# First FFN of a two-block transformer kernel: half of the first weight panel ahead of x's second half, gate products first, modulation products half a step later

## The chip, the cores and the metric

The kernel runs on one NeuronCore of a Trainium2 chip. The metric is the device time of one execution in microseconds, taken as the median of several runs. TensorE, VectorE, ScalarE, GpSimd and the sync engine (SP) each run their own instruction list and meet only at semaphores; weights come from HBM through DMA queues that SP and GpSimd feed.

## The reference, cut to what matters

Two blocks over a sequence of 512 tokens with 1024 features. Only the first FFN and the modulation vector of the second block are touched:

```python
# block 1, first step; D_MODEL 1024, D_FF 2816
x = x + 0.5 * swiglu(rms_norm(x, ffn1_norm), ffn1_w_gate, ffn1_w_up, ffn1_w_down)
# swiglu(h): (silu(h @ w_gate) * (h @ w_up)) @ w_down
...
# block 2 scales and shifts by six 1024-wide parts of one vector
mod = silu(c) @ w_mod + b_mod          # w_mod: 1024 x 6144
```

The rest (gated MLP and differential attention, a second FFN, then the second block with a state-space part, windowed attention and a conv FFN) follows in one chain and is the same in both kernels.

## The kernel before

Features lie on partitions: x is 8 tiles (k = 0 to 7) of 128 features by 512 tokens. Every float32 operand of a product is split into a rounded part (`hi`) and the rest (`lo`), and each product is three TensorE products: hi by hi, hi by lo and lo by hi. Weights come in panels of 128 x 2048 (1 MB): SP loads one into one of two `w_raw` buffers, ScalarE casts it to `w_hi`, VectorE subtracts for `w_lo` (semaphore `w_split`), and only then may SP load the panel after next (`load`, L492: panel n waits for `w_split` of n - 1).

**Start.** SP issues x in four quarters of 256 features (L568), then gate panel 0 in two halves (L530, L531), then up panel 1 (L532), then many small parameter loads, panel 2, the small spread loads of `load_spread` (L510), and panel 3. TensorE transposes x tile by tile into PSUM banks 2 to 5 (L2521); VectorE copies each tile to `x` (L1663); ScalarE makes `h_hi` = x times the norm's gain (L828), VectorE `h_lo` (L1376). The norm's root is applied later, to the products. Between the transposes and the products TensorE multiplies ones (`idle_products`, L2507). ScalarE casts the first half of panel 0 behind six of the eight `h_hi` tiles (L920), and the second half behind the seventh (L923).

**First FFN.** It has 11 steps of two panels (gate, then up), each panel 48 products of 512 columns: 8 k, 2 output tiles, 3 terms. `first_gate` (L2353) runs panel 0 by terms: 16 hi by hi, 16 hi by lo, 16 lo by hi; then `first_sums` (L2525) transposes parameter rows, multiplies the position table and sums the squares of x for the root. Later panels go through `by_k` (L2336). VectorE's step (L1567 to L1594) is: scale two gate tiles by the root, split the next gate panel, multiply silu by two up tiles, split the next up panel, make two `hid_lo` tiles.

**Modulation.** Beside the first FFN, the first 8 of 12 groups of mod (512 columns each) are made. GpSimd loads eight tiles of w_mod per group into four buffers (`group`, L623): a buffer is loaded again once VectorE has used it (`mod_step`). VectorE multiplies and adds (`modulation`, L1539) at the head of each step: for step 0 four products ahead of the root and four behind the split of panel 2, for the others all eight. At the end of the step TensorE adds up the partitions with 4 small products (8 records, L2394), for which it waits until all eight are done. GpSimd starts group 0's last four loads only behind `cleared` (L647), which waits for the position table's copy on VectorE (L1674, behind `first_sums`) and clears a tile; the table copies of `tables` (L655) follow in the same queue.

`PHASES` cuts the steps into loops: 0; 1 to 6; 7; 8 to 10. The same `swiglu`, `gate_up` and `modulation` serve the second FFN, with a column of conditions on its name.

Of the kernel before, what the change touches and what calls it, by code (L numbers as in the profile page):

```python
# [33 lines left out]
P = 128  # L34
T = 512
TB = T // P
# [41 lines left out]
PHASES = {"ffn1": ((0, 1, True, None), (1, BESIDE_STEPS - 1, True, None), (BESIDE_STEPS - 1, BESIDE_STEPS, True, None), (BESIDE_STEPS, GU_STEPS, False, None)),  # L78
# [57 lines left out]
def build(nc, inp, rel_onehot, out):  # L136
# [13 lines left out]
    with ExitStack() as ctx:  # L150
# [135 lines left out]
        SW_BEFORE = [sum(len(k) for k in SW_BLOCKS[:u]) for u in range(len(SW_UNITS) + 1)]  # L286

# [203 lines left out]
        def _(sp):  # L491
# [32 lines left out]
            def load_ffn(name, gate, up, gate_col, up_col, down):  # L524
# [3 lines left out]
                if base == 0:  # L528
                    first_panel = panel(w_raw, 0, KD, PC)
                    sp.dma_start(first_panel[:, 0:KD // 2], gate_v[:, 0:KD // 2, 0:PC]).then_inc(S("w0_tables_landed"), 16)  # L530
                    sp.dma_start(first_panel[:, KD // 2:], gate_v[:, KD // 2:, 0:PC]).then_inc(S("w_landed0"), 16)  # L531
# [35 lines left out]
            for q in range(D // PC):  # L567
                sp.dma_start(x_in[:, :, q * PC:(q + 1) * PC], x_v[:, :, q * PC:(q + 1) * PC]).then_inc(S(f"x_landed{q}"), 16)  # L568
# [194 lines left out]
        def _(act):  # L763
# [153 lines left out]
            first_hi = lambda ks: scaled_hi("n1", "start", lambda k: gain1[:, k:k + 1], ks)  # L917
# [424 lines left out]
        def _(dve):  # L1342
# [210 lines left out]
            def swiglu(name):  # L1553
                base = BASE[name]
                setup = (s5_matrices, s5_first_angles, s5_second_angles, s5_powers)
                for start, stop, mods, extra in PHASES[name]:
                    if start == BESIDE_STEPS:
# [9 lines left out]
                    with dve.Fori(start, stop) as i:  # L1567
                        if start == 0:
                            modulation(i + MOD_AT[name], i, range(MOD_SLOTS))
                            refined_root({"ffn1": "n1", "ffn2": "n2"}[name])  # L1570
                        elif mods:
                            modulation(i + MOD_AT[name], i, range(KD if name == "ffn1" else MOD_SLOTS))
# [9 lines left out]
                        if start == 0 and name == "ffn1":  # L1582
                            modulation(i + MOD_AT[name], i, range(MOD_SLOTS, KD))
# [77 lines left out]
            for k in range(KD):  # L1661
                dve.wait_ge(S("x_t"), k + 2)
                dve.tensor_copy(x[:, k, :], B[2 + k % 4][:]).then_inc(S("x_turned"), 1)  # L1663
                if k == 3:
                    scaled_lo("n1", lambda k: gain1[:, k:k + 1], (0, ))
            scaled_lo("n1", lambda k: gain1[:, k:k + 1], range(1, KD))
            split(0)
            split(1)
            dve.wait_ge(S("rows_t"), 3)
# [569 lines left out]
        def _(pe):  # L2239
# [113 lines left out]
            def first_gate(n, banks, h_name, between):  # L2353

                wh, wl = panel(w_hi, n, KD, PC), panel(w_lo, n, KD, PC)
                if h_name == "n1":
                    pe.wait_ge(S("w0_begun"), 1)
                else:
                    pe.wait_ge(S("w_hi_done"), n + 1)
                for wait, h in ((ready_hi, h_hi), (ready, h_lo)):  # L2360
                    for k in range(KD):
                        wait(h_name)(k)
                        if h_name == "n1" and h is h_hi and k == KD // 2:
                            pe.wait_ge(S("w_hi_done"), n + 1)
                        for t, bank in enumerate(banks):
                            pe.matmul(bank[:], wh[:, k, t * P:(t + 1) * P], h[:, k, :], start=k == 0 and h is h_hi, stop=False)  # L2366
                if h_name != "n1":
                    between()
# [6 lines left out]
                if h_name == "n1":  # L2375
                    between()

            def gate_up(name, h_name, free, sums=None):

                base = BASE[name]  # L2380
                for start, stop, mods, extra in PHASES.get(name, ((1, GU_STEPS, False, None),)):
                    with pe.Fori(start, stop) as i:
# [752 lines left out]
```

## Time and profile before

| | us |
|---|---|
| median of 3 runs (lowest, highest) | 1749.19 (1748.01, 1749.32) |
| profiled execution, its own time | 1748.42 |
| its span, first to last record | 1746.8 |
| TensorE busy | 1736.5 (99%) |
| VectorE, ScalarE, GpSimd busy | 1057.1, 736.4, 199.4 |
| first weight product starts | 13.97 |
| step 1 of the first FFN starts | 39.43 |

Times in the rows are microseconds from the start of the span; PE is TensorE (PEld its weight loads), DVE is VectorE, ACT is ScalarE, POOL is GpSimd, and SPq is SP's sequencer, where DMA issues stand. A float32 transpose or product of 128 columns is recorded as two instructions or as one according to its kind, so counts of the trace and of the code can differ by a factor of two. A matmul's recorded duration includes its way through the array, so 16 in a row take less than 16 durations.

### The profile page before, as it was taken

The page shows a single profiled execution, that of the slowest core. Times are in us where ns is not written, and L with a number is a line of the kernel's source. Part 1 is how long each engine was busy: PE and PEld are TensorE (multiplying, and loading weights), DVE is VectorE, ACT ScalarE, POOL GpSimd, SP SyncE. Part 2 cuts the span into 40 slices and gives each one's busy share as a digit, 9 for nine tenths or more (in the row PEclk, how much of TensorE's full clock was granted, in tenths as well). Part 3 has the DMA queues.
Part 4 walks back from the last instruction along what each step waited for, and adds up shares of the span by engine and source line. Part 5 has one row for each costly group of instructions (what it writes and reads, how often), then busy time and mean ns, then how long its engine had stood idle before and what let it go on. Part 6 is the DMA issues. An engine that isn't in the chain of part 4 may idle for free.

```text
span 1746.8 us, 23624 instructions
## 1 busy us (share of the span) xinstructions
PE 1736.5 (99%) x8907; PEld 1425.0 (82%) x8907; DVE 1057.1 (61%) x1623; ACT 736.4 (42%) x1045; POOL 199.4 (11%) x249
## 2 busy tenths in 40 slices
PE   9999999999999999999999999999999999999999
PEld 7888888888888777788888888888987888888887
DVE  6666536655564667655788854346587665555423
ACT  5322223333444887623333322224576455555321
POOL 2222001140000000004510120130003300000000
PEclk9999999999999999999999999999999999999999
DMA  7877422343223211223754562325131222222331
GB/s 246 251 227 226 139 75 82 102 150 103 97 65 104 66 56 49 73 97 97 235 181 135 161 175 66 103 96 193 49 147 49 97 97 96 96 96 84 102 116 67
DMA packets 169701, 207.18 MB, mean 119 GB/s; under 512 B 18516, under 2 KB 144850, under 8 KB 169106
## 3 DMA queue, kind: packets, MB, share of 16 engines
q1 hardware_dynamic: 142882, 161.97, 28.6%
q0 software_dynamic: 12752, 38.81, 7.1%
q10 hardware_dynamic: 13984, 5.27, 1.4%
q8 instruction: 55, 0.90, 0.2%
q14 instruction: 28, 0.23, 0.0%
HBM read 190.56 MB, written 17.56 MB: 119 GB/s over the span
## 4 chain that ended last, share of the span: by engine, by line
PE 94%; DVE 3%; DMA 2%; ACT 1%; issue 0%; POOL 0%; SPq 0%; ACTq 0%; DVEq 0%
PE bank L2348 41%; PE bank L2275 35%; PE bank L2666 5%; PE bank L2690 1%; PE bank L2787 1%; DMA w_raw<-in_w_in 1%; PE bank L2243 1%; PE bank L2366 1%; PE bank L2700 1%; PE bank L2560 1%; PE bank L3048 1%; PE bank L2840 0%; PE bank L3060 0%; PE bank L2909 0%; PE bank L2372 0%; PE bank L2854 0%
## 5 line engine op out<-in xcount | busy, mean ns | idle before, releaser
L778 ACT CAST w_hi<-w_raw 128x2048 fp32r<-128x2048 f32 x154 | 294.1, 1910 | 722.4 <-PE bank L2348 355.5
L1356 DVE TENSOR_TENSOR w_lo<-w_raw,w_hi 128x2048 fp32r<-128x2048 f32 x156 | 364.7, 2338 | 348.0 <-ACT w_hi L778 347.3
L2348 PE MATMUL bank<-h_hi,w_hi 128*128 128x512 f32 x1024 | 400.7, 391 | 0.5 <-DVE h_lo L1397 0.2
L2348 PE MATMUL bank<-h_hi,w_lo 128*128 128x512 f32 x1024 | 398.6, 389 | 0.0
L2348 PE MATMUL bank<-h_lo,w_hi 128*128 128x512 f32 x1024 | 315.4, 389 | 0.0
L2348 PEld LDWEIGHTS bank<-h_hi,w_hi 128*128 128x128 f32 x1024 | 192.2, 188 | 44.6 <-issue 3.3
L2348 PEld LDWEIGHTS bank<-h_lo,w_hi 128*128 128x128 f32 x1024 | 192.2, 188 | 40.2
L2348 PEld LDWEIGHTS bank<-h_hi,w_lo 128*128 128x128 f32 x1024 | 192.2, 188 | 39.2
L2275 PE MATMUL bank<-hid_hi,w_hi 128*128 128x512 f32 (+1 forms) x450 | 173.3, 385 | 0.0
L2275 PE MATMUL bank<-hid_lo,w_hi 128*128 128x512 f32 (+1 forms) x450 | 172.9, 384 | 0.0
L2275 PE MATMUL bank<-hid_hi,w_lo 128*128 128x512 f32 (+1 forms) x450 | 172.9, 384 | 0.0
L670 POOL TENSOR_TENSOR tmp<-x 128x512 f32<-128x512 f32 x28 | 43.3, 1548 | 623.6 <-DVE x L1978 312.2
L2275 PEld LDWEIGHTS bank<-hid_hi,w_hi 128*128 128x128 f32 x450 | 84.5, 188 | 17.0
L2275 PEld LDWEIGHTS bank<-hid_hi,w_lo 128*128 128x128 f32 x450 | 84.5, 188 | 16.9
L2275 PEld LDWEIGHTS bank<-hid_lo,w_hi 128*128 128x128 f32 x450 | 84.5, 188 | 16.6
L2275 PE MATMUL bank<-w_hi,h_hi 128*128 128x512 f32 (+1 forms) x240 | 91.2, 380 | 0.3 <-DVE w_lo L1356 0.3
L2275 PE MATMUL bank<-w_hi,h_lo 128*128 128x512 f32 (+1 forms) x240 | 90.1, 375 | 0.0
L2275 PE MATMUL bank<-w_lo,h_hi 128*128 128x512 f32 (+1 forms) x240 | 90.0, 375 | 0.0
L1550 DVE SCALAR_TENSOR_TENSOR mod_acc<-mod_raw,small,mod_acc 128x512 f32<-128x512 f32 x84 | 63.1, 751 | 27.3 <-DMA mod_raw<-in_w_mod 22.6
L627 POOL DMA_DIRECT2D mod_raw<-in_w_mod x96 | 52.0, 543 | 171.2 <-DVE mod_acc L1547 123.2
L1592 DVE TENSOR_TENSOR tmp<-tmp,bank 128x512 f32<-128x512 f32 x44 | 28.2, 683 | 70.7 <-PE bank L2348 70.7
L2203 DVE SCALAR_TENSOR_TENSOR tmp<-bank,vec,tmp 128x511 f32<-128x511 f32 x88 | 63.8, 745 | 6.4 <-DVE tmp L2203 1.7
(506 smaller groups left out, 2690.9 us busy)
## 6 DMA issues: line engine op xcount, KB each, us to landing
w_raw<-in_w_in SPq DMA_DIRECT2D x29, 1024.0 KB, 5.1
mod_raw<-in_w_mod POOLq DMA_DIRECT2D x96, 256.0 KB, 4.8
w_raw<-in_ffn_w_up SPq DMA_DIRECT2D x22, 1024.0 KB, 5.6
w_raw<-in_w_up SPq DMA_DIRECT2D x22, 1024.0 KB, 5.1
w_raw<-in_ffn_w_gate SPq DMA_DIRECT2D x21, 1024.0 KB, 6.7
w_raw<-in_ffn_w_down SPq DMA_DIRECT2D x16, 768.0 KB, 4.3
w_raw<-in_ffn_w_down SPq DMA_DIRECT2D x16, 640.0 KB, 3.9
w_raw<-in_w_out SPq DMA_DIRECT2D x8, 1024.0 KB, 4.9
```

The lines of the kernel that those rows point to most:

```text
L627: pool.dma_start(mod_raw[:, k % MOD_SLOTS, :], wm[:, k, bass.ds(i * T + first * T, T)])\
L670: done(pool.tensor_tensor(tmp[:, min(k, 1), :], x[:, k, :], x[:, k, :], ALU.mult))
L778: act.copy(w_hi[i % 2][:], w_raw[i % 2][:]).then_inc(S("w_hi_done"), 1)
L1356: dve.tensor_tensor(w_lo[s][:], w_raw[s][:], w_hi[s][:].bitcast(F32), ALU.subtract).then_inc(S("w_split"), 1)
L1550: ins = dve.scalar_tensor_tensor(mod_acc[:], mod_raw[:, k % MOD_SLOTS, :], small[:, k:k + 1], mod_acc[:], ALU.mult, ALU.add)
L1592: dve.tensor_tensor(tmp[:, 2 + t, :], tmp[:, t, :], B[2 + t][:], ALU.mult).then_inc(S("hid"), 1)
L2203: dve.scalar_tensor_tensor(y[:, back:], up[:, :T - back], col_at(f"conv_w_2:{2 - back}", i * 2, KF * half + t), y[:, back:], ALU.mult, ALU ...
L2243: mm = pe.matmul(out_ap, stationary, moving, start=first and i == 0, stop=last and i == len(terms) - 1)
L2275: mm = pe.matmul(out_ap, stationary, moving, start=first and i == 0, stop=last and i == total - 1)
L2348: mm = pe.matmul(bank[:], w[:, k, at], h[:, k, :], start=k == first and part == 0 and i == 0, stop=k == last and part == 1)
L2366: pe.matmul(bank[:], wh[:, k, t * P:(t + 1) * P], h[:, k, :], start=k == 0 and h is h_hi, stop=False)
L2666: mm = pe.matmul(beside_bank(name, t)[:], stationary, moving, start=j == 0, stop=j == 3 * k - 1)
```

## The change

SP: x comes as quarters (0, 1), then x's second half in one load; the first half of panel 0 is issued ahead of x's second half, the second half of the panel behind it. The four transposed tiles of x's second half get banks 4 to 7. ScalarE makes `h_hi` straight from the transposed tile's bank; VectorE copies the tile to `x` after it. The panel's first half is cast after four tiles instead of six, and its `lo` half gets a subtraction of its own. TensorE transposes four tiles, runs the first half's hi by hi products, transposes the other four, and runs the rest of panel 0; the six idle products behind the transposes go (the eight at the very start stay). Panel 1's hi by hi products come ahead of `first_sums`.

Modulation in the first FFN: group 0's first four products stay ahead of step 0, but behind `split(1)`, and the other four come at the end of step 0. Groups 1 to 7 come behind the gate panel's split of their step instead of at its head. TensorE's small products of group g move from the end of step g to the middle of step g + 1, behind its gate panel.

```diff
-PHASES = {"ffn1": ((0, 1, True, None), (1, BESIDE_STEPS - 1, True, None), (BESIDE_STEPS - 1, BESIDE_STEPS, True, None), (BESIDE_STEPS, GU_STEPS, False, None)),
+PHASES = {"ffn1": ((0, 1, True, None), (1, 2, True, None), (2, BESIDE_STEPS, True, None),
+                   (BESIDE_STEPS, BESIDE_STEPS + 1, False, None), (BESIDE_STEPS + 1, GU_STEPS, False, None)),
...
+        X_QUARTERS = ((0, 2), (2, 4), (4, KD))
+        def x_bank(k):
+            return B[k if k >= 4 else 2 + k]
...
+                    load_x(0)
+                    load_x(1)
+                    sp.dma_start(gate_panel[:, early], gate_v[:, early, 0:PC]).then_inc(S("w0_tables_landed"), 16)
+                    load_x(2)
+                    sp.dma_start(gate_panel[:, late], gate_v[:, late, 0:PC]).then_inc(S("w_landed0"), 16)
...
+                for k in ks:
+                    act.wait_ge(S("x_t"), k + 2)
+                    act.activation(h_hi[:, k, :], x_bank(k)[:], ACT.Identity, scale=gain1[:, k:k + 1]).then_inc(S("norm_hi"), 1)
...
-            first_hi(range(6))
+            first_hi(range(4))
             act.wait_ge(S("w0_tables_landed"), 16)
-            act.copy(w_hi[0][:, 0:PANEL // 2], w_raw[0][:, 0:PANEL // 2]).then_inc(S("w0_begun"), 1)
-            first_hi((6, ))
+            act.copy(w_hi[0][:, early], w_raw[0][:, early]).then_inc(S("w0_begun"), 1)
+            first_hi(range(4, KD))
             act.wait_ge(S("w_landed0"), 16)
-            act.copy(w_hi[0][:, PANEL // 2:], w_raw[0][:, PANEL // 2:]).then_inc(S("w_hi_done"), 1)
-            first_hi((7, ))
+            act.copy(w_hi[0][:, late], w_raw[0][:, late]).then_inc(S("w_hi_done"), 1)
...
                         if start == 0:
-                            modulation(i + MOD_AT[name], i, range(MOD_SLOTS))
+                            if name == "ffn2":
+                                modulation(i + MOD_AT[name], i, range(MOD_SLOTS))
...
                         split(i * 2 + (base + 2), base)
-                        if start == 0 and name == "ffn1":
-                            modulation(i + MOD_AT[name], i, range(MOD_SLOTS, KD))
+                        if mods and start and name == "ffn1":
+                            modulation(i + MOD_AT[name], i)
...
                         split(i * 2 + (base + 3), base + 1)
                         for t in range(2):
                             hid_lo_of(name, i, t, 2 + t)
+                        if start == 0 and name == "ffn1":
+                            modulation(i + MOD_AT[name], i, range(MOD_SLOTS, KD))
...
+            first_x(range(4))
+            first_lo(range(4))
+            dve.wait_ge(S("w0_begun"), 1)
+            low_part(slice(0, PANEL // 2), "w_lo_begun")
+            first_x(range(4, KD))
+            first_lo(range(4, KD))
+            dve.wait_ge(S("w_hi_done"), 1)
+            low_part(slice(PANEL // 2, PANEL), "w_split")
             split(1)
+            modulation(0, 0, range(MOD_SLOTS))
...
+            def first_ffn_step():
+                early, late = range(KD // 2), range(KD // 2, KD)
+                turned_x(early)
+                pe.wait_ge(S("w0_begun"), 1)
+                first_products(0, early, w_hi, h_hi, ready_hi)
+                turned_x(late)
+                first_products(0, early, w_hi, h_lo, ready)
+                pe.wait_ge(S("w_lo_begun"), 1)
+                first_products(0, early, w_lo, h_hi, ready_hi)
+                pe.wait_ge(S("w_hi_done"), 1)
+                first_products(0, late, w_hi, h_hi, ready_hi)
+                first_products(0, late, w_hi, h_lo, ready)
+                pe.wait_ge(S("w_split"), 1)
+                first_products(0, late, w_lo, h_hi, ready_hi)
+                pe.wait_ge(S("w_hi_done"), 2)
+                pe.wait_ge(S("x_turned"), 3)
+                first_products(1, range(KD), w_hi, h_hi, ready_hi)
+                first_sums()
+                first_products(1, range(KD), w_hi, h_lo, ready)
+                pe.wait_ge(S("w_split"), 2)
+                first_products(1, range(KD), w_lo, h_hi, ready_hi)
...
+                def modulation_rows(step, behind, first, last):
+                    pe.wait_ge(S("mod_step"), step * MOD_STEPS + ((MOD_AT[name] + behind + 1) * MOD_STEPS + MOD_SLOTS))
...
+                    if name == "ffn1" and start == 0:
+                        first_ffn_step()
+                        continue
...
+                            if name == "ffn1" and half == 0 and start <= BESIDE_STEPS:
+                                modulation_rows(i, -1, start == 1, start == BESIDE_STEPS)
...
-            idle_products(6, ones[:], 7)
```

`first_products(half, ks, w, h, wait)` issues for each k of ks one product for each of the half's two banks, each 512 columns wide, waiting for `h`'s tile k; `turned_x(ks)` transposes the tiles ks and for k = 4 and 5 waits until VectorE has copied tile k - 2.

## Rows read from the trace of the kernel before

**Rows 1.** The granted clock of TensorE in 40 slices of the span, in tenths of full speed.
```profile
PEclk9999999999999999999999999999999999999999
```

**Rows 2.** TensorE's longest wait after the start: who for whom, total, times, longest.
```profile
PE bank L2366 <- ACT w_hi L920: 0.9, 1, 0.9
```

**Rows 3.** Chain of waits, first 320 us: start, length, what.
```profile
13.97 7.55 PE bank L2366 x32
...
25.16 0.27 PE bank L2531 x3
...
38.04 0.76 DVE mod_acc L1550
38.84 0.43 PE bank L2394 x8
...
61.83 21.99 PE bank L2348 x96
```

**Rows 4.** Timeline of TensorE: first product of panel 1, step 1's gate and up panel.
```profile
27.01 0.47 PE L2348 MATMUL bank<-h_hi,w_hi 128*128 128x512 f32 x1
...
39.43 0.49 PE L2348 MATMUL bank<-h_hi,w_hi 128*128 128x512 f32 x1 [0.16 <-issue]
...
50.43 0.39 PE L2348 MATMUL bank<-h_hi,w_hi 128*128 128x512 f32 x1
```

**Rows 5.** TensorE's transposes grouped, 5.9 to 9.3 us, then 9.8 to 11.5 us.
```profile
L2521 PE MATMUL bank<-ident,x_in 128*128 128x128 f32 x16 | 3.7, 424 | 0.0
...
L2521 PE MATMUL bank<-ident,x_in 128*128 128x128 f32 x16 | 2.3, 306 | 0.0
```

**Rows 6.** Timeline of ScalarE and VectorE, 5.9 to 27 us.
```profile
9.67 0.69 DVE L1663 COPY x<-bank 128x512 f32<-128x512 f32 x1 [0.16 <-PE bank L2521]
...
12.89 1.03 ACT L920 CAST w_hi<-w_raw 128x1024 fp32r<-128x1024 f32 x1
```

**Rows 7.** VectorE and ScalarE grouped, 7 to 26 us: busy, mean ns, idle before.
```profile
L1376 DVE SCALAR_TENSOR_TENSOR h_lo<-x,gain,h_hi 128x512 fp32r<-128x512 f32 x8 | 5.5, 743 | 0.0
...
L828 ACT ACTIVATE h_hi<-x,gain 128x512 fp32r<-128x512 f32 x8 | 5.7, 720 | 2.1 <-DVE x L1663 1.7
```

**Rows 8.** One load each, issue to landing: x's third quarter with its second; panel's first half.
```profile
L568 SPq DMA_DIRECT2D x_in<-in_x x2: 494/497/500, 1.5 to 2.1; - x2
...
DMA to landing us min/median/max: 4.5/5.5/6.6
...
L530 SPq DMA_DIRECT2D w_raw<-in_ffn_w_gate x1: 593/593/593, 3.2 to 3.2; - x1
...
DMA to landing us min/median/max: 8.5/8.5/8.5
```

**Rows 9.** Timeline of SP: loads of panels 2 and 3.
```profile
20.27 0.40 SPq L500 DMA_DIRECT2D w_raw<-in_ffn_w_gate  x1
...
28.81 2.71 SPq L500 DMA_DIRECT2D w_raw<-in_ffn_w_up  x1
```

**Rows 10.** Panel 3, then panel 2: their loads' time from issue to landing.
```profile
DMA to landing us min/median/max: 13.6/13.6/13.6
...
DMA to landing us min/median/max: 8.2/8.2/8.2
```

**Rows 11.** Timeline of VectorE behind panel 3, and of four modulation products later.
```profile
44.34 2.29 DVE L1356 TENSOR_TENSOR w_lo<-w_raw,w_hi 128x2048 fp32r<-128x2048 f32 x1 [4.36 <-ACT w_hi L778]
46.55 1.28 DVE L1426 TENSOR_TENSOR hid_lo<-tmp,hid_hi 128x512 fp32r<-128x512 f32 x2
...
71.98 3.12 DVE L1550 SCALAR_TENSOR_TENSOR mod_acc<-mod_raw,small,mod_acc 128x512 f32<-128x512 f32 x4 [2.18 <-DMA mod_raw<-in_w_mod]
```

**Rows 12.** Timeline of GpSimd: group 0's last four loads.
```profile
28.55 2.14 POOL L627 DMA_DIRECT2D mod_raw<-in_w_mod  x4 [0.30 <-POOL zero L650]
```

**Rows 13.** DMA queues, 35 to 39 us: q0 is GpSimd's, q1 SP's; packets, MB, share.
```profile
q0 software_dynamic: 356, 1.08, 72.3%
q1 hardware_dynamic: 434, 0.44, 31.7%
```

More of the change, by code:

```diff
@@ L1660, in _, with first_x, first_lo, low_part @@
             dve.tensor_copy(gain1[:], B[6][:, 0:2 * KD]).then_inc(S("x_turned"), 1)
[L1661 to L1667, printed above, removed]
+            def first_x(ks):
+                for k in ks:
+                    dve.wait_ge(S("norm_hi"), k + 1)
+                    dve.tensor_copy(x[:, k, :], x_bank(k)[:]).then_inc(S("x_turned"), 1)
+            def first_lo(ks):
+                for k in ks:
+                    dve.wait_ge(S("x_turned"), k + 2)
+                    scaled_lo("n1", lambda k: gain1[:, k:k + 1], (k, ))
+            def low_part(at, signal):
+                dve.tensor_tensor(w_lo[0][:, at], w_raw[0][:, at], w_hi[0][:, at].bitcast(F32), ALU.subtract).then_inc(S(signal), 1)
+            first_x(range(4))
[6 more added lines that the diff above has]
+            low_part(slice(PANEL // 2, PANEL), "w_split")
             split(1)
+            modulation(0, 0, range(MOD_SLOTS))
             dve.wait_ge(S("rows_t"), 3)
@@ L2362, in first_gate @@
                         wait(h_name)(k)
-                        if h_name == "n1" and h is h_hi and k == KD // 2:
-                            pe.wait_ge(S("w_hi_done"), n + 1)
                         for t, bank in enumerate(banks):
                             pe.matmul(bank[:], wh[:, k, t * P:(t + 1) * P], h[:, k, :], start=k == 0 and h is h_hi, stop=False)
-                if h_name != "n1":
-                    between()
+                between()
                 pe.wait_ge(S("w_split"), n + 1)
@@ L2374, in first_gate, with turned_x @@
                             mm.then_inc(S("pe_done"), 2)
-                if h_name == "n1":
-                    between()
+            def turned_x(ks):
+                for k in ks:
+                    pe.wait_ge(S(f"x_landed{min(k // 2, 2)}"), 16)
+                    if k in (4, 5):
+                        pe.wait_ge(S("x_turned"), k)
+                    for b in range(TB):
+                        mm = pe.transpose(x_bank(k)[:, b * P:(b + 1) * P], x_in[:, b, k * P:(k + 1) * P], ident[:])
+                    mm.then_inc(S("x_t"), 1)
@@ new lines, in first_products @@
+            def first_products(half, ks, w, h, wait):
+                weights = panel(w, half, KD, PC)
+                for k in ks:
+                    wait("n1")(k)
+                    for t in range(2):
+                        mm = pe.matmul(B[2 * half + t][:], weights[:, k, t * P:(t + 1) * P], h[:, k, :], start=k == 0 and w is w_hi and h is h_hi,
+                                       stop=k == KD - 1 and w is w_lo)
+                        if k == KD - 1 and w is w_lo:
+                            mm.then_inc(S("pe_done"), 2)
@@ L2378, in gate_up @@
             def gate_up(name, h_name, free, sums=None):
                 base = BASE[name]
+                def modulation_rows(step, behind, first, last):
+                    pe.wait_ge(S("mod_step"), step * MOD_STEPS + ((MOD_AT[name] + behind + 1) * MOD_STEPS + MOD_SLOTS))
+                    for j in range(4):
+                        mm = pe.matmul(B[6][32 * j:32 * j + 32, 0:P], row_of[:], mod_acc[:, j * P:(j + 1) * P], start=first, stop=last)
+                    mm.then_inc(S("mod_acc_free"), 1)
@@ L2542, in swiglu_free @@
                 return free
-            gate_up("ffn1", "n1", swiglu_free("ffn1"), first_sums)
+            gate_up("ffn1", "n1", swiglu_free("ffn1"))
             down("ffn1")
```

37 lines of the change are left out of this document (12 added, 25 removed).

## The prediction

> **What bounds the kernel now.** Look first at the waits of TensorE and at the granted clock: TensorE is busy for 99% of the span (the table above) at full clock [rows 1], and after its start nothing stops it for more than 0.9 us at a time [rows 2]. So a change of order can only win what TensorE waits for, and the chain of waits of the first 60 us says where that is. Before 13.97 us it goes through x's copies and casts. From there to 38 us it is weight products, with `first_sums` in between. Then come four modulation products on VectorE, 0.76 us each, and the eight small products that waited for them [rows 3]. Step 1 starts at 39.43 and its up panel at 50.43 [rows 4], and from then on each step is 96 products in 21.99 us and 0.36 us of small products without a gap [rows 3]. The whole argument is therefore one number: by how much does step 1's up panel start earlier or later than 50.43? What is late there is late at the end.
>
> **The earlier start.** The first product waits for the cast of half a panel, 12.89 to 13.92 [rows 6], behind six `h_hi` tiles. Now four go ahead of it, and ScalarE reads the bank itself. The fourth tile is in its bank at 9.67, where VectorE's copy starts today [rows 6]; plus 0.72 for `h_hi` [rows 7] and 1.03 for the cast: 11.4, first product 11.5. The half panel must be there by 10.4. It takes the slot of x's third quarter, which landed 6.6 us after 2.1, so at 8.7; with today's 8.5 us from issue [rows 8] it would be 10.6. Both bounds cost at most 0.2. Gain 2.5 us.
>
> What is paid for it: the 16 transposes of x's second half now stand between products. In the first 3.4 us of transposes sixteen take 3.7 us, later sixteen take 2.3, tail of 0.3 included [rows 5]: I take 2.0. The 96 products of step 0 go at the pace of the 48 from 13.97 to 25.16 [rows 3], 0.227 each after the first's latency, 21.9 in all. `first_sums` takes 25.16 to 27.01 [rows 3, 4], 1.9. So the up panel ends at 11.5 + 2.0 + 21.9 + 1.9 = 37.3, against 38.0 now. The small products no longer stand there, nor does the wait for them: step 1 starts at 37.4 instead of 39.43, a gain of 2.0. Inside it everything is covered: the second half's `h_hi` (16.9), its cast (18.0) and panel 1's (19.9) are made before TensorE wants them (19.2, 19.2 and 24.5).
>
> Behind `first_sums` (end 30.0) come the root, its refinement, two scaled gates and the split of panel 2, about 6.7 us together as today from 27.3 to 35.4 less the modulation products that stood in between. That is 36.7, just ahead of 37.4. If this cover goes, the time lost is hidden by the next paragraph's wait.
>
> **The new wait.** Step 1's gate panel takes 11.0 us [rows 4], so TensorE is through it at 48.4. There it now waits for all eight products of group 0, and VectorE makes the last four of them only behind step 0's split of panel 3 and two `hid_lo` tiles. Today they are made at 35.5 to 38.8, ahead of that split. So a load whose split had 3.8 us of slack (done at 46.6 [rows 11], wanted at 50.43) comes onto the path with the products behind it: panel 3. Behind the waiting products in TensorE's queue stands the whole up panel; behind that split in VectorE's queue stand step 1's gates too.
>
> When does panel 3 land? Its load is the last of a row of issues on SP: panel 2 goes out at 20.27, the moment panel 0's `w_split` comes, and panel 3 8.54 us later, with the small spread loads between [rows 9]. VectorE's new order up to that `w_split`: the copies of tiles 0 to 3 wait for `h_hi` and end at 9.67 + 0.72 + 0.69 = 11.1; then VectorE is never idle: four `h_lo` at 0.68 (5.5 / 8) [rows 7], half a split 1.15, four copies 2.8, four `h_lo` 2.7, half a split 1.15: 21.6. Panel 2 goes out 1.3 us later than now and panel 3 at 30.1. It took 13.6 us to land [rows 10], so 43.7.
>
> From landing to TensorE: cast 1.94 (42.4 to 44.34), split until `hid_lo` at 46.55, so 2.2, two `hid_lo` 1.2, four products 3.1 [rows 11] with 0.1 ahead, and 0.6 from the last product to the first weight product behind the small ones, as now (38.80 to 39.43) [rows 3, 4]. That is 9.1. The up panel of step 1 starts at 43.7 + 9.1 = 52.8 instead of 50.43: a loss of 2.4 us. TensorE stands still from 48.4 to 52.2, nearly 4 us, where it stood 0.7 before.
>
> Bounds of the load's 13.6. Below: panel 2's took 8.2 [rows 10]; panel 3 then lands at 38.3 and nothing waits. Above: in 35 to 39 us GpSimd's queue carried 1.08 MB and SP's 0.44 [rows 13], so panel 3 gets a quarter or less of the engines while group 0's last loads and the table copies run. GpSimd's four loads started at 28.55, ahead of panel 3 [rows 12]. They wait for the table's copy behind `first_sums`, now 3 us later, so up to 2 us more of them meets the panel, at three quarters of the engines: 1 to 1.5 us more. On the other side, group 1's loads, which took part of the engines before 42.4, now wait for VectorE. I take 13.6, the same load's own row, since both shifts are small and opposed.
>
> **The rest of the modulation move.** Steps 1 to 7 keep all their instructions. VectorE's eight products come behind a split of 2.3 instead of ahead of two gates; with their wait for loads they took 8 us and end within a microsecond of the up panel's end, and what needs them, the small products, has another 11 us. The scaled gates come earlier. I cost this at nothing; the cover is half a step, and each microsecond beyond it would count seven times. The small products are as many as before (8 groups, 0.36 us each in the chain). GpSimd's group and table queue moves with VectorE, half a step later, and its last copies have over a step until ScalarE waits for them. The cut of the loops costs nothing: the chain shows no gap at the cuts of today.
>
> **Sum.** Step 1's up panel +2.4, the rest 0. The profiled execution took 1748.42, so 1750.8 by it; the median of the runs shown is 0.8 above that execution, which would make 1751.6. I predict 1751.2.
>
> **Rivals.**
>
> A. *Not slower: panel 3 lands early.* The new wait is nothing if the panel has landed by 48.4 + 0.4 - 9.1 = 39.7, and costs less than the gain if by 41.3, which is 11.2 us from issue. For it: GpSimd's loads start later and group 1's do not come, so the panel could have the engines to itself at first. Against: it is itself queued behind the spread loads, which now run 1.3 us later, and 13.6 included more than 3 us before its data moved at all. Then the up panel starts at 48.8, a gain of 1.6: 1747.2 with half the offset to the median.
>
> B. *The clock is low at the start.* The six idle products and the copies' pace kept TensorE at work to 13 us. Now it stands still from 9.9 to 11.5. The transposes ran at half pace at first (0.23 each) and at full pace from about 9.6 [rows 5], so at the 1.2 GHz level and then at 2.4. If the rise comes later in the new order, the first eight products take 1.8 us more and the late transposes 1.6 more; copies, `w_split` and panel 3 move by some 2 us: +4.5, 1753.3. For it: the rise came only at the very end of the stretch of work that is now all there is before the pause. Against: that stretch itself is unchanged.
>
> C. *The clock falls in the new wait.* No row here has TensorE idle for 4 us, and no row has the clock fall [rows 1, 2]. If it falls, some products of the up panel take twice 0.227; 8 to 16 of them are 1.8 to 3.6 us: +5, 1753.8.
> The Trainium skill ("TensorE: Matmul & The Clock Gate", "Part 1: The HAM clock gate") says that the array's clock is let up by sustained work and goes back to 1.2 GHz in idleness. It speaks for B and C; that rows 5 show the rise agrees with it, and no row here shows the fall.
>
> D. *The panel is later still*, by GpSimd's loads meeting it or by the half panel of the start landing late: +4, 1752.8.
>
> **Chances.** Forecast 0.50; A 0.20; B 0.12; C 0.08; D 0.10. What a measurement of this kernel can tell from no change is 0.2%, 3.5 us: under 1745.7 or over 1752.7. No case reaches the first, and a misjudged gain gets 0.03. Over the second lie most of B and C, half of D and a little of the forecast's spread: 0.22. The rest, 0.75, is within. The range takes in A and half of B to D: 1746.8 to 1753.9; the forecast's own is 1750 to 1752.5.
>
> **What would show it.** In the profile after: the first product at 11.5 (later with the half panel's landing as releaser: the load order did not help; transposes and products at twice their spacing: B). Step 1's gate panel at 37.4. Panel 3's issue at 30.1 and its cast at 43.7. A wait of 3 to 4 us of TensorE's small products for the modulation product on VectorE, once, and none in steps 2 to 8. If that wait is missing I am wrong in the sign; if it recurs in each step, in the size.

## The result, and the profile after

The changed kernel takes 1755.38 us (median of 6 executions, 1750.80 to 1758.88); the kernel before, run beside it on the same chip, 1747.87. The ratio is 1.0043, with a 95% interval of 1.0034 to 1.0053: slower by 7.5 us, where 1751.2 was predicted and, with a chance of 0.75, a difference of less than 0.2%. All times below are medians of such executions; kernels that were run together share the runs of the kernel before.

The six executions differ in one more thing: their mean granted clock is 0.996 to 0.999, and the longest are those with the lowest clock. The kernel before keeps 1.000 nearly always. The execution that was profiled is the fastest, 1750.80 with a span of 1749.3; a second profile of the same kernel took 1754.18. Both are shown, as their difference is part of the answer.

TensorE's waits in the first profile (who for whom, total, times, longest), against 0.9 after the start in [rows 2]:

```profile
PE bank L2917 <- issue: 3.1, 1, 3.1
PE bank L2428 <- ACT w_hi L942: 1.9, 1, 1.9
PE bank L2593 <- POOL ones L630: 1.3, 1, 1.3
PE bank L2464 <- DVE mod_acc L1571: 1.1, 1, 1.1
```

The last row is the wait that was predicted. The first was in no step of mine: 3.1 us in which nothing that the profile shows was waited for. TensorE's timeline (start, length, what, idle before and releaser):

```profile
5.28 3.04 PE L2419 MATMUL bank<-ident,x_in 128*128 128x128 f32 x16
10.18 3.15 PE L2428 MATMUL bank<-h_hi,w_hi 128*128 128x512 f32 x8 [1.85 <-ACT w_hi L942]
13.12 2.52 PE L2419 MATMUL bank<-ident,x_in 128*128 128x128 f32 x16
...
37.58 0.39 PE L2391 MATMUL bank<-h_hi,w_hi 128*128 128x512 f32 x1
49.71 0.43 PE L2464 MATMUL bank<-mod_acc,row_of 128*32 128x128 f32 x8 [1.08 <-DVE mod_acc L1571]
1282.38 3.91 PE L2917 MATMUL bank<-uc,wb 64*64 64x64 f32 x127
1289.37 0.27 PE L2917 MATMUL bank<-uc,wb 64*64 64x64 f32 x1 [3.08 <-issue]
```

These rows answer to [rows 4, 5]. The first product starts at 10.18 instead of 13.97, step 1 at 37.58 instead of 39.43. The last two rows are over a millisecond later, in a part that the change does not touch: 128 small products (L2917) run without a gap in the kernel before, and here the last of them stands alone behind the 3.1 us. The same place in the kernel before (L2840), where the last of the 128 is sent between the first two of the next group:

```profile
1282.90 4.12 PE L2840 MATMUL bank<-uc,wb 64*64 64x64 f32 x127
1286.81 0.27 PE L2898 MATMUL bank<-tz,uc 64*64 64x128 f32 x1
1286.86 0.22 PE L2840 MATMUL bank<-uc,wb 64*64 64x64 f32 x1
```

The chain of waits for the place that the prediction turns on (start, length, what; it answers to [rows 3, 10, 11]):

```profile
29.11 11.84 DMA w_raw<-in_ffn_w_up
...
40.97 1.92 ACT w_hi L793
...
42.92 1.07 DVE w_lo L1377
...
45.12 1.28 DVE hid_lo L1447 x2
...
48.90 0.76 DVE mod_acc L1571
...
49.71 0.43 PE bank L2464 x8
50.13 21.98 PE bank L2391 x96
```

The path is the predicted one, link by link. Here the panel came after 11.84 us and the up panel starts at 50.13, 0.3 before the old 50.43. The chain passes `PE bank L2402`, the end of the first FFN, at 261.43 in the kernel before and at 261.19 (L2488) in this execution: up to there nothing is lost. All of its 2.5 us come from the wait at 1286. In the kernel's second profile the same chain reads:

```profile
28.07 14.01 DMA w_raw<-in_ffn_w_up
...
50.83 0.65 PE bank L2464 x8
51.48 23.88 PE bank L2391 x96
75.72 21.99 PE bank L2391 x96
```

and its windows (stretch in us, its length, TensorE's busy time and instructions, granted clock, mean busy share of the DMA engines, GB/s):

```profile
42.00:46.40 4.40, 4.34 (x20) 1.00 0.33 108
46.40:50.80 4.40, 0.00 (x0) 0.76 0.75 236
50.80:54.80 4.00, 3.97 (x16) 0.50 0.75 266
54.80:58.80 4.00, 4.00 (x17) 0.91 0.84 259
```

Here the panel needs 14.01 us and TensorE stands still for 4.49 us. From 48.7, still inside this wait, the granted clock is 0.50, the 1.2 GHz level, for 6.8 us: the 96 products take 23.88 us instead of the 21.99 of [rows 3]. This execution passes the end of the first FFN at 264.43, 3.0 late, and loses another 2.8 at 1289 to 1293. So there are two losses of about 3 us, of which I had priced the first at 2.4 and the second at nothing.

### The profile page after: what moved, and what is told of

Same layout as the page of the kernel before. It is cut to its first block, busy times and chain, and to the rows that moved or that the text cites. A ratio compares the mean times of both kernels' runs of the same rounds, so it can differ in the third digit from the quotient of the medians.

```text
span 1749.3 us, 23597 instructions
## 1 busy us (share of the span) xinstructions
PE 1735.7 (99%) x8895; PEld 1424.1 (81%) x8895; DVE 1057.7 (60%) x1624; ACT 735.9 (42%) x1045; POOL 199.2 (11%) x249
## 4 chain that ended last, share of the span: by engine, by line
PE 94%; DVE 3%; ACT 1%; DMA 1%; issue 1%; SPq 0%; POOL 0%; DVEq 0%; POOLq 0%
PE bank L2391 40%; PE bank L2318 35%; PE bank L2743 5%; PE bank L2767 1%; PE bank L2864 1%; PE bank L2286 1%; PE bank L2777 1%; DMA w_raw<-in_ffn_w_up 1%; PE bank L2637 1%; PE bank L3125 1%; PE bank L2832 0%; PE bank L2917 0%; PE bank L3137 0%; PE bank L2986 0%; PE bank L2931 0%
## 5 line engine op out<-in xcount | busy, mean ns | idle before, releaser
L2391 PE MATMUL bank<-h_hi,w_hi 128*128 128x512 f32 x1008 | 394.3, 391 | 0.4 <-DVE h_lo L1418 0.4
L2391 PE MATMUL bank<-h_hi,w_lo 128*128 128x512 f32 x1008 | 392.4, 389 | 0.0
L2391 PE MATMUL bank<-h_lo,w_hi 128*128 128x512 f32 x1008 | 310.4, 389 | 0.0
L2391 PEld LDWEIGHTS bank<-h_lo,w_hi 128*128 128x128 f32 x1008 | 189.2, 188 | 39.5
L1600 DVE TENSOR_TENSOR tmp<-bank,rstd 128x512 f32<-128x512 f32 x44 | 28.3, 686 | 55.9 <-PE bank L2391 48.0
```

Of the source, the lines that this page charges most:

```text
L1600: dve.tensor_tensor(tmp[:, t, :], B[t][:], rstd[:], ALU.mult).then_inc(S("gate_scaled"), 1)
L2391: mm = pe.matmul(bank[:], w[:, k, at], h[:, k, :], start=k == first and part == 0 and i == 0, stop=k == last and part == 1)
```

## The experiments

**Is it repeatable?** The changed kernel once more, beside the third set.

> The changed kernel itself once more, for a second profile and more times. Clock theory: wherever its mean clock is 0.996 to 0.998, the profile shows the clock at half behind the wait of the small products (about 50 us), behind the issue wait at the state-space inputs (about 1288 us), or both, for some 7 us each; none elsewhere but in the pause of the start. Median 1754 to 1757, 6 to 10 us above before. Rival (the slow executions are slow somewhere else): a wait or a low clock in another place.

Measured: 1754.82, ratio 1.0048 [1.0034, 1.0061], clocks 0.996 to 0.998. Its profile is the second one above, and shows both losses in one execution.

**Is it the pause at the start?** Two runs: the changed kernel with eight idle products between the first four tiles and the first weight product (e1, "filled"); and the reverse, the old kernel without its six (e2).

```diff
# e1_filled, against the changed kernel
                 turned_x(early)
+                idle_products(8, ones[:], 7)
                 pe.wait_ge(S("w0_begun"), 1)
# e2_before_no_idle, against the kernel before
-            idle_products(6, ones[:], 7)
```

> The changed kernel with one line more: eight idle products of ones (16 records) behind the transposes of x's first half, where TensorE stood still from 8.3 to 10.2 us. Clock theory (the pause lets TensorE's granted clock fall to half while the first products run; executions with a mean clock of 0.996 to 0.998 had it low for longer): mean clock 0.999 to 1.000 in every execution, the spread of 8 us gone, time 4 to 7 us below the changed kernel's 1755.4, so within 3 us of before. Wait theory (the small products' wait for panel 3 is what is long in the slow executions): the time stays at 1753 to 1757 with the same spread. Layout theory (an issue wait of 3.1 us at the state-space inputs, L2917 of the changed kernel, because its instructions lie elsewhere): that wait stays, as the code is only a few instructions longer, and keeps the time 3 us above before.

> The kernel before without its six idle products between the transposes and the first product: the only thing done is that TensorE pauses from 11.6 to 14.0 us. Clock theory: clock under 1.000 in most executions, time 2 to 7 us above before, with a wide spread. Wait and layout theories: nothing else moves, so the same as before, within 0.5 us.

Measured: filled, 1757.18, 1.0053 [1.0039, 1.0066], clocks still 0.996 to 0.998; the old kernel without its six, 1747.76, 1.0000 [0.9991, 1.0009]. The pause is not the cause of the loss. The clock is full through the start of the filled kernel's profile, and its low clock shows in and behind the two other waits:

```profile
PE bank L2465 <- DVE mod_acc L1571: 4.2, 1, 4.2
PE bank L2918 <- issue: 3.5, 1, 3.5
```

For 6.8 us from 49.5 and for 6.8 us from 1291.9 it is granted half. That it is no faster than the changed kernel although its start is better was the first sign that the place of the code counts.

**Which half of the change?** The new start with the old modulation, and the old start with the new modulation (both with the phases that go with the modulation).

```diff
# e3_start_only, against the changed kernel: groups at the head of their step again
-                            if name == "ffn2":
-                                modulation(i + MOD_AT[name], i, range(MOD_SLOTS))
+                            modulation(i + MOD_AT[name], i, range(MOD_SLOTS))
...
                         first_ffn_step()
+                        modulation_rows(0, 0, True, False)
# e4_mod_only, against the kernel before: small products behind the next gate panel
+                            if name == "ffn1" and half == 0 and 1 <= start <= BESIDE_STEPS:
+                                modulation_rows(i, -1, start == 1, start == BESIDE_STEPS)
```

> The changed start (load order, transposes in two halves, panel 0 by halves, panel 1's first products ahead of the sums, no idle products) with the modulation as before: four products ahead of the root, four behind the split of panel 2, small products at the end of their own step. Clock theory: 1753 to 1757 with the wide spread and clocks of 0.996 to 0.999, as the pause is there. Wait theory: there is no wait for panel 3 any more, so about before's time, 0 to 1 us less.

> The start of before with the changed modulation: group 0's last four products behind the split of panel 3, the others behind the gate panel's split, small products in the middle of the next step. Clock theory: clock 1.000 and a narrow spread; only the wait for panel 3 counts: step 1 starts 1.4 us earlier, its up panel at 51 to 52, so 0 to +2 us against before. Wait theory: +4 to +8 us, as in the changed kernel, with its spread.

Measured: start only, 1752.19, 1.0025 [1.0016, 1.0035]; modulation only, 1753.92, 1.0036 [1.0024, 1.0048]. Either half alone loses, and for different reasons. The time of start only lies between what the two theories expected, so neither was right about it. It waits 4.2 us for group 0 ahead of step 1, gets half the clock for 3.4 us from 39.5, and has no wait for issue:

```profile
PE bank L2459 <- DVE mod_acc L1570: 4.2, 1, 4.2
```

So the start gives nothing while step 1 stands behind group 0's small products: the modulation has to move for it. Modulation only waits 0.8 us for group 0 and is 1.3 us ahead of the kernel before at the end of the first FFN (260.17 against 261.43). Its loss is at the other end:

```profile
1281.96 3.56 PE L2850 MATMUL bank<-uc,wb 64*64 64x64 f32 x115
...
1288.91 1.00 PE L2850 MATMUL bank<-uc,wb 64*64 64x64 f32 x13 [3.38 <-issue]
```

The gap now stands behind 115 products, not 127. What these kernels differ in at this place is only how many instructions TensorE's list has ahead of it: against the kernel before, modulation only has 198 more, the changed kernel 173 more, the filled one 205 more. The gap stands behind 115, 127 and 111 records: one record earlier for two instructions more. In the traces TensorE's instructions are fetched in packets of 16384 bytes, so a block's border should lie at a fixed count of the list, and whatever cuts a loop once more moves it. The next two runs test this.

**Is it the place of the code alone?** The kernel before with nothing changed but one more cut of TensorE's loop list (198 instructions more ahead of that place); and the changed kernel with three more cuts (782 more than the kernel before).

```diff
+CUTS = {"ffn1": (10,), "ffn2": ()}                 # e5_before_shifted
+CUTS = {"ffn1": (7, 10), "ffn2": (10,)}            # e6_after_shifted
...
-                for start, stop, mods, extra in PHASES.get(name, ((1, GU_STEPS, False, None),)):
+                for start, stop, mods, extra in PE_PHASES.get(name, ((1, GU_STEPS, False, None),)):
```

`PE_PHASES` is `PHASES` with each range cut at these steps. TensorE executes the same products in the same order.

> The kernel before with TensorE's list alone made longer: the loop over steps 8 to 10 of the first FFN is cut in two (8, 9 and 10), so one more unrolled step stands in the list, and everything behind it lies 198 instructions later (the changed kernel's lies 173 later). The same instructions run in the same order. Layout theory (the issue wait at the state-space inputs comes from where the list's blocks end, and the clock falls behind it): TensorE waits 3.0 to 3.5 us for issue at L2840 inside the second run of 128 small products, about 13 before its end as in e4_mod_only, the granted clock falls behind it in part of the executions, and the time is +3 to +7 us. Wait theory (only the modulation's waits count): no change, within 0.5 us.

> The changed kernel with three more cuts of TensorE's loops (the first FFN's steps 2 to 7 cut before 7, its last two steps and the second FFN's last three cut once each), so that the second block's code lies 782 later than in before, 14 more than three blocks of 256. The same instructions in the same order as in the changed kernel. Layout theory: no issue wait at the state-space inputs, time 3 to 6 us below the changed kernel's 1755.4, so 1749 to 1752; what is left is the wait for panel 3 and the clock behind it. Wait theory: 1755.

Measured: the kernel before, shifted, 1752.32, 1.0026 [1.0016, 1.0036]; 5.0 us for a loop cut. The changed kernel, shifted, 1751.42, 1.0016 [1.0007, 1.0025], 3.4 to 4.0 us under the changed kernel's two medians. (By the ratios, which take in two low executions of the eleven, 1747.87 and 1746.63, it is 4.7 or more.) In the shifted old kernel TensorE's timeline and windows (columns as above) show the gap and what follows it:

```profile
1282.16 3.59 PE L2845 MATMUL bank<-uc,wb 64*64 64x64 f32 x115
...
1289.07 1.01 PE L2845 MATMUL bank<-uc,wb 64*64 64x64 f32 x13 [3.32 <-issue]
```

```profile
1281.00:1285.00 4.00, 4.00 (x106) 1.00 1.02 341
1285.00:1289.00 4.00, 0.75 (x25) 0.91 0.65 208
1289.00:1293.00 4.00, 3.93 (x54) 0.50 0.02 4
1293.00:1297.00 4.00, 4.00 (x45) 0.74 0.00 0
```

TensorE stands still for 3.3 us, and for 6.8 us from 1288.3, shortly before it goes on, the clock is half. In the changed kernel, shifted, no wait for issue is left, but the wait for group 0 is 3.9 us and the clock is half for 6.8 us from 49.0.

**Why does the fetch take so long?** When TensorE comes to that place, the DMA engines are full (1.02 above). SP has queued 2 MB of `ca_out` and 2 MB for `w_out` behind 2 MB of `tz`. The run is the shifted old kernel again, with the `ca_out` load, and with it the `w_out` loads behind it, held back until that block of products is through:

```diff
+            sp.wait_ge(S("bu"), 2)
             sp.dma_start(ca_out[:], ca_dram[:]).then_inc(S("ca_landed"), 16)
```

> e5_before_shifted (before with a list 198 instructions longer) with one wait more on SP: the 2 MB load of ca_out, and the two 1 MB weight panels queued behind it, start only when TensorE is through the second run of 128 small products. Data theory (the list's next block of 256 instructions comes by DMA and is late because 6 MB of loads are in its way): the issue wait of 3.3 us at L2845 is gone, under 0.5 us; in its place the products that need ca_out wait some us for it, so the time is no better than e5's. Rival (the block is late by the list's form alone, whatever the data): the wait of 3.3 us stays where it is.

Measured: the gap is 0.31 us, at the same record.

```profile
1283.58 3.56 PE L2846 MATMUL bank<-uc,wb 64*64 64x64 f32 x115
...
1287.46 0.62 PE L2846 MATMUL bank<-uc,wb 64*64 64x64 f32 x13 [0.31 <-issue]
...
1295.99 5.38 PE L2915 MATMUL bank<-ca_out,tmp 64*64 64x128 f32 x64 [3.34 <-DMA ca_out<-chunk_outputs]
```

The fetches themselves are in the traces. TensorE's instruction packet of 16384 bytes stands in the queue q8: first the shifted old kernel, 1286 to 1287 us, then this run, 1285 to 1286 us.

```profile
q8 instruction: 1, 0.02, 7.0%
...
q8 instruction: 1, 0.02, 5.8%
```

In the first TensorE stops at 1285.75; the packet starts only at 1286.65, 0.9 us later, and lands at 1287.77, and the products go on at 1289.07. In the second the packet starts at 1285.09, 2.1 us ahead of the stop. Counted from the start of the 128 products, the packet moves 3.0 us later with the loads in the queues (4.5 against 1.5 us), which is the difference of the two gaps (3.32 less 0.31). In all seven profiles with a gap 1.3 to 1.5 us pass between the packet's landing and the next product. Why the transfer starts late, whether the fetch is asked for late or stands in line behind the loads, no record shows.

The time did not fall (1753.53, 1.0035 [1.0022, 1.0049]), as the last row says: the load held back is now waited for itself, 3.3 us, again with half the clock behind it. So the cause of the gap is shown, but holding the load back is no remedy. The Trainium skill ("Runtime: NRT & Kernel Launch", "Instruction fetch mechanics") says that the sequencer refills its buffer in 16 KiB blocks by a DMA queue of its own, at a cost that is mostly hidden. The traces agree with the block and with the queue; with idle DMA engines 0.31 us is nearly hidden, with full ones the 3.1 to 3.5 us are not.

**Is the rest group 0 behind panel 3?** The changed kernel with the last four products of group 0 ahead of panel 3's split.

```diff
+                        if start == 0 and name == "ffn1":
+                            modulation(i + MOD_AT[name], i, range(MOD_SLOTS, KD))
                         split(i * 2 + (base + 3), base + 1)
                         for t in range(2):
                             hid_lo_of(name, i, t, 2 + t)
-                        if start == 0 and name == "ffn1":
-                            modulation(i + MOD_AT[name], i, range(MOD_SLOTS, KD))
```

> The changed kernel with group 0's last four modulation products on VectorE ahead of the split of panel 3 instead of behind it and the two hid_lo tiles (VectorE is idle from 38.8 to 42.9 us there). Its code is as long as the changed kernel's. Wait theory: TensorE's small products wait for nothing, step 1's up panel starts at 48.7 instead of 50.1 to 53, and the clock no longer falls there: 2 to 4 us below the changed kernel. Layout theory: the issue wait of 3.1 us stays at the state-space inputs, with the clock's fall behind it in part of the executions, so not under 1749.

Measured: 1750.27, 1.0013 [1.0004, 1.0022]: 4.6 to 5.1 us less than the changed kernel, with the wait for issue (3.4) still in. In its profile no wait for group 0 is left, and the up panel starts at 49.04. Group 0 behind the split costs the changed kernel 4.6 to 5.1 us, more than the 2 to 4 that were expected.

**How much of it is the clock?** The changed kernel as in e6, with TensorE kept at work on idle products while it waits for group 0, and with one more cut, so that the list (1034 more) again has no border there.

```diff
+CUTS = {"ffn1": (7, 10), "ffn2": (9, 10)}
...
+                            if name == "ffn1" and half == 0 and start == 1:
+                                idle_products(14, ones[:])
                             if name == "ffn1" and half == 0 and start <= BESIDE_STEPS:
                                 modulation_rows(i, -1, start == 1, start == BESIDE_STEPS)
```

> e6_after_shifted (1751.4; no issue wait at the state-space inputs) with fourteen idle products ahead of the small products that wait for group 0 in step 1, so TensorE multiplies ones for 3.4 us of its wait of 3.9. The code of the second block lies 10 instructions later than in before modulo 256. If half of what this wait costs is the clock that falls behind it (6.8 us at half, 3.4 us lost): 1748 to 1749, mean clock 0.999 to 1.000. If the wait alone costs: the same as e6_after_shifted, or a little more.

Measured: 1749.28, 1.0010 [1.0001, 1.0019], against 1751.42 for e6: 2.1 us less. TensorE is not earlier for it: the idle products fill 3.1 us in the profile and the up panel starts at 51.81 against 51.09 in e6, but the products behind run at full pace. The same stretch, without the idle products (e6) and with them (e11):

```profile
46.00:50.00 4.00, 0.53 (x3) 0.88 0.72 217
50.00:54.00 4.00, 3.56 (x15) 0.50 0.89 306
```

```profile
46.00:50.00 4.00, 4.00 (x28) 1.00 0.47 131
50.00:54.00 4.00, 4.00 (x32) 1.00 1.04 364
```

In the chains the 96 products behind the wait take 24.28 us in e6 and 22.01 in e11, whose step 1 begins no earlier. So about 2 us of what group 0's wait costs are the clock's, and the rest is the wait itself.

**All together.** Eight idle products, the four modulation products early, and TensorE's list cut so that no border falls there (1028 instructions more); and the same without the idle products (996 more).

```diff
+CUTS = {"ffn1": (6, 7, 10), "ffn2": (10,)}
...
+                idle_products(8, ones[:], 7)               # e8_all only
...
                         # and group 0's last four ahead of split(panel 3), as in e7
```

> The changed kernel with the three put together: eight idle products in the pause of the start, group 0's last four products ahead of the split of panel 3, and TensorE's loops cut so that the second block's code lies 4 instructions later than in before, modulo 256. If the issue wait with its clock, the wait for panel 3 with its clock, and the pause of the start are the whole of it: mean clock 1.000 in every execution, no wait of TensorE over 1 us, step 1's up panel at 48 to 48.7 instead of 50.43, and 1.5 to 2.5 us below before. If something else of the change costs time: above before still.

> e8_all without its eight idle products, so TensorE pauses for 1.9 us in the start again. Clock theory: the clock falls to half from about 11 us on in part or all of the executions, mean clock 0.999 in these; the first products take twice as long and the whole is 0.5 to 2 us above e8_all's 1745.5. Rival (the idle products are worth nothing, as e2_before_no_idle found of the six in before): the same as e8_all within 0.3 us.

Measured: 1745.52 (1744.88 to 1746.33, 11 executions), 0.9985 [0.9976, 0.9994], clock 1.000 in all of them; without the idle products 1746.63, 0.9994 [0.9985, 1.0003], clock 0.999 in 5 of 11. The first is faster than both kernels, if by less than the 0.2% that count here. Its start:

```profile
7.70 1.95 PE L2599 MATMUL bank<-ones 128*128 128x128 f32 x16
10.01 2.12 PE L2433 MATMUL bank<-h_hi,w_hi 128*128 128x512 f32 x8 [0.35 <-ACT w_hi L947]
```

and its chain:

```profile
35.96 10.88 PE bank L2396 x48
46.84 0.36 PE bank L2470 x8
47.20 12.92 PE bank L2396 x56
```

The up panel starts at 47.20 against 50.43 in [rows 4]: the 3.2 us that the start really gains. The end of the first FFN is 3.2 us earlier too (258.26 against 261.43), the span is 2.6 shorter. The median is only 1.8 under that of the kernel before, as the profiled execution of the latter (1748.42) was 1.1 above the median of the runs beside e8, and that of e8 only 0.3 above its own.

| kernel | us | ratio [95%] | wait for group 0 | wait for issue |
|---|---|---|---|---|
| changed | 1755.38, 1754.82 | 1.0043 [1.0034, 1.0053], 1.0048 [1.0034, 1.0061] | 1.1, 4.5 | 3.1, 3.1 |
| e6, list shifted | 1751.42 | 1.0016 [1.0007, 1.0025] | 3.9 | none |
| e7, four early | 1750.27 | 1.0013 [1.0004, 1.0022] | none | 3.4 |
| e10, both | 1746.63 | 0.9994 [0.9985, 1.0003] | none | none |
| e8, both and filled | 1745.52 | 0.9985 [0.9976, 0.9994] | none | none |

e6 and e7 each take one loss away, e10 both. The two effects add, as far as the medians tell: 3.6 (e7 less e10) and 4.8 (e6 less e10) make 8.4, and from e10 to the changed kernel it is 8.2 to 8.8.

## Why the prediction was wrong

It said 1751.2 and the kernel takes 1755.38. **The step that failed** is the sentence "The cut of the loops costs nothing: the chain shows no gap at the cuts of today". I looked for the cost of a cut at the cut. It lies 1.25 ms later: the new phases and the new start lengthen TensorE's list by 173 instructions, the border of a 16384-byte block comes to lie in a dense run of small products while 6 MB of loads fill the DMA engines, and TensorE stands for 3.1 us. In neither profile of the changed kernel does the clock fall there, but in e1, e4 and e5 it does; a mean clock of 0.996 in some of the changed kernel's executions, as in the profile of e1 that has both falls, suggests that it does in these too. Price: 5.0 us where it is alone (e5 against the kernel before), 3.4 to 4.0 within the change (e6 against the changed kernel's medians). That is the larger part of the miss. The miss is also larger than 1755.38 less 1751.2: I had taken 1748.8 for the kernel before, and its runs here give 1747.87, so +2.4 was forecast and +7.5 measured. That the changed kernel without the shift stands at 1751.42, next to the 1751.2 predicted, is in part luck: it is 4.1 over its own before. The profile before held no number for the shift, but it has instruction packets among its DMA queues, and any change of the list's length moves every border: the upper bound should not have been zero.

**A term was mis-sized**: the new wait. Its mechanism was right in each link: from the panel's landing to the up panel I worked out 9.1 us, and they are 9.2 (40.95 to 50.13) and 9.4 (42.08 to 51.48). I priced it at +2.4 against the kernel before. With the shift taken out the net is +4.1 (e6, 1751.42, over 1747.34), and with TensorE kept at work in the wait +1.9 (e11, 1749.28, over 1747.40). The difference of the two is the clock, and without it the forecast would have been near. The profiles split it the same way: the up panel starts 1.1 us late in the changed kernel's second and 0.7 in e6 (51.48 and 51.09 against 50.43), less than the 2.4 of the forecast, since the start gained more than I had given it; the clock adds 1.9 and 2.3 (23.88 and 24.28 against 21.99). I had the clock as rival C, with a chance of 0.08. In the four profiles with a wait for group 0 of 3.9 to 4.5 us (the changed kernel's second, e1, e3, e6) the clock fell each time, 0.4 to 2.2 us before the wait was over; the first profile waited only 1.1 us, and it did not. The Trainium skill's rule ("TensorE: Matmul & The Clock Gate", "Part 1: The HAM clock gate") that idleness takes the clock back to 1.2 GHz agrees with these four, and deserved more weight than the absence of a row.

**Point by point.** *Step 1 at 37.4*: 37.58, right, but by errors that cancel: the first product came at 10.18, not 11.5, since its cast began at 9.08, where I had taken 10.4; the transposes and products of 11 to 14 us ran at half the clock in that profile, which ate it. In the second, at full clock, the first product is at 9.51 and step 1 at 35.30. *Panel 3's issue at 30.1*: 29.11 (28.07 in the second profile), early as the cast was. *13.6 us to land*: 11.84 and 14.01; in e1 14.12, in e6 14.25, in e3 14.6 and in e8 and e10 14.5. The value was good and the first profile the exception, and the bounds were right to be wide. *Rival A*, the panel early: it needed 11.2 us and got 11.84 once; no profile shows it. *Rival B*, the low clock at the start: not as the late rise that I described, but as a fall behind the pause, for 3.4 us from 11.0, it is in the first profile, in those of e7 and e11 too, and not in the second, e3, e6 or e10. Filling it is worth 1.1 us where nothing else is late (e8 against e10), not 4.5. *Rival D*, later still: the landing of 14.0 to 14.6 is 0.4 to 1.0 us of it. *The rest of the modulation move at nothing*: right. No profile has the wait in steps 2 to 8, and e8, which has the same order there, is faster than the kernel before.

**The sum, as the runs give it.** With both waits out and the pause filled, start and new order gain 1.8 (e8). The pause costs 1.1 (e10 less e8), group 0 behind panel 3 4.8 (e6 less e10; 4.6 to 5.1 by e7), the place of the code 3.6 (e7 less e10; 3.4 to 4.0 by e6): 1.1 + 4.8 + 3.6 - 1.8 = 7.7, against 7.5 measured. These are differences of medians, each good to some tenths of a microsecond at best, so the agreement is closer than it had to be.

## What to carry to other kernels

When a change alters the number of instructions of the engine that bounds a kernel, give its code's new place a price that is not zero, and test it alone: shift the unchanged kernel's list by about the same count. A wait of TensorE of about 4 us costs more than its length, here about 2 us more for the clock, so look for work that can stand in it. Before moving work behind a load's split, ask what the load's own landing varies by: here 11.8 to 14.6 us in the variants of the changed kernel, and never within the 11.2 us from issue that would have kept the change from losing.

## What the runs showed of the hardware

- An instruction fetch stalls TensorE for 3.1 to 3.5 us where a block's border falls into 128 small products, 0.03 us apart, beside full DMA engines (1.02 of them busy over 4 us, then 0.65, in e5), and for 0.31 us at the same record when they are idle. The packet started 0.6 to 1.0 us after TensorE had stopped in the first case, and 2.1 us before the stop in the second. The gap was there with 173, 198 and 205 instructions more, and not with 0, 782, 996, 1028 and 1034 more, nor with 24 and 25 less. Between these the place was not tried.
- With equal waits the clock may fall or not. At the wait for issue it fell to 0.50 in e1, e4 and e5 (waits of 3.5, 3.4 and 3.3 us) and it stayed 1.00 in e7 (3.4) and in both profiles of the changed kernel (3.1). Behind a pause of 1.8 us it stayed full in e2; behind one of 1.9 to 2.4 near 10 us it fell in three of seven profiles. What decides it was not found. It fits the spread of the changed kernel's executions, over 8 us at mean clocks of 0.996 to 0.999, and of e8's, over 1.5 at 1.000, but only the profiled executions show where the clock fell.
- The windows of the changed kernel's first profile show that fall coming behind the first products, not with the pause:

```profile
8.30:10.20 1.90, 0.05 (x2) 1.00 1.04 386
10.20:11.00 0.80, 0.80 (x4) 0.97 1.09 364
11.00:14.00 3.00, 3.00 (x11) 0.50 1.09 349
14.00:15.00 1.00, 1.00 (x9) 0.82 0.71 206
```
